# Two more units ahead of the first level of the linear attention

## What is computed

```python
def step(s, inp):
    qc, kc, vc, gc = inp
    b = jnp.cumsum(gc, axis=2)
    rel = jnp.where(lower, b[:, :, :, None, :] - b[:, :, None, :, :], -jnp.inf)
    a = jnp.einsum('bhid,bhjd,bhijd->bhij', qc, kc, jnp.exp(rel))
    o = jnp.einsum('bhid,bhde->bhie', qc * jnp.exp(b), s) + jnp.einsum('bhij,bhje->bhie', a, vc)

def _merge(o_att, o_gla, r, glu, gates, p):
    o_gla = _rmsnorm(o_gla, p['gla_norm']).transpose(0, 2, 1, 3).reshape(B, L, GLA_V)
    y_gla = (o_gla * jax.nn.silu(r)) @ p['w_gla_o']
    g_att, g_gla, g_conv = jnp.split(jax.nn.sigmoid(gates), N_BRANCH, axis=-1)
    return (g_att * y_att + g_gla * y_gla + g_conv * y_conv) @ p['w_out']
```

## Time and profile before

| | us |
|---|---|
| median of 3 runs | 3085.33 (3079.8 to 3087.47) |
| the profiled execution, its time | 3074.02 |
| its span, from first to last instruction | 3072.2 |
| TensorE busy | 2873.4 (94%) |
| VectorE busy | 2202.6 (72%) |
| ScalarE busy | 1507.7 (49%) |
| granted TensorE clock, mean | 0.953 of full speed |

### The profile page before, as it was taken

How to read it: one execution, slowest core, us unless ns; L and a number is a source line. 1 busy time by engine, 2 the same in 40 slices (tenths; PEclk the granted TensorE clock), 3 DMA queues, 4 the chain that set the end, 5 groups by cost and what they waited for, 6 DMA issues and landing times.

```text
span 3072.2 us, 54612 instructions
## 1 busy us (share of the span) xinstructions
PE 2873.4 (94%) x21460; PEld 2728.1 (89%) x21460; DVE 2202.6 (72%) x3789; ACT 1507.7 (49%) x3102; POOL 0.2 (0%) x4
## 2 busy tenths in 40 slices
PE   8999999999899999989998999998999889997998
PEld 7998889899889879989988997897998779995998
DVE  6976777678799876866657898867666655566655
ACT  3644345444555434545465653454544455555554
POOL 0000000000000000000000000000000000000000
PEclk7999989899999989989999999998999899998999
DMA  7543434388543233435533423335453326541554
GB/s 265 155 158 102 142 121 157 130 279 274 190 157 111 96 104 130 145 116 179 182 125 112 150 77 110 110 118 189 151 185 117 110 64 191 186 140 48 163 181 156
DMA packets 123191, 451.50 MB, mean 147 GB/s; under 512 B 13728, under 2 KB 15776, under 8 KB 122192
## 3 DMA queue, kind: packets, MB, share of 16 engines
q1 hardware_dynamic: 108704, 393.35, 39.5%
q10 hardware_dynamic: 14256, 54.86, 5.3%
HBM read 447.10 MB, written 1.05 MB: 146 GB/s over the span
## 4 chain that ended last, share of the span: by engine, by line
PE 64%; DVE 23%; ACT 5%; DMA 5%; issue 2%; SPq 0%; ACTq 0%; DVEq 0%
PE lin L467 14%; PE lin L468 14%; PE lin L469 14%; DVE w_lo L1588 6%; DVE arena L1759 5%; DMA w_raw<-in_stream 4%; PE lin L517 3%; PE aux L580 2%; ACT w_hi L1023 2%; PE aux L712 1%; DVE rstd L1613 1%; PE aux L571 1%; PE aux L645 1%; PE aux L624 1%; PE lin L480 1%
## 5 line engine op out<-in xcount | busy, mean ns | idle before, releaser
L1588 DVE TENSOR_TENSOR w_lo<-w_raw,w_hi 128x1024 fp32r<-128x1024 f32 x722 | 876.3, 1221 | 334.0 <-ACT w_hi L1023 330.2
L467 PE MATMUL lin<-h_hi,w_hi 128*128 128x256 f32 x3584 | 1033.3, 288 | 7.4 <-ACT arena L1280 3.7
L468 PE MATMUL lin<-h_lo,w_hi 128*128 128x256 f32 x3584 | 1022.0, 285 | 0.0
L469 PE MATMUL lin<-h_hi,w_lo 128*128 128x256 f32 x3584 | 1021.7, 285 | 0.0
L1023 ACT ACTIVATE w_hi<-w_raw 128x512 fp32r<-128x512 f32 x1446 | 828.5, 623 | 320.1 <-DMA w_raw<-in_stream 228.4
L467 PEld LDWEIGHTS lin<-h_hi,w_hi 128*128 128x128 f32 x3584 | 696.4, 194 | 13.8 <-ACT arena L1280 5.9
L468 PEld LDWEIGHTS lin<-h_lo,w_hi 128*128 128x128 f32 x3584 | 696.4, 194 | 0.4
L469 PEld LDWEIGHTS lin<-h_hi,w_lo 128*128 128x128 f32 x3584 | 695.7, 194 | 0.0
L467 PE MATMUL lin<-s_hi,w_hi 128*128 128x256 f32 x1392 | 411.9, 296 | 17.1 <-DVE s_lo L1674 13.7
L468 PE MATMUL lin<-s_lo,w_hi 128*128 128x256 f32 x1392 | 403.6, 290 | 0.0
L469 PE MATMUL lin<-s_hi,w_lo 128*128 128x256 f32 x1392 | 403.0, 290 | 0.0
(11 more groups left out here) (269 smaller groups left out, 3963.9 us busy)
## 6 DMA issues: line engine op xcount, KB each, us to landing
w_raw<-in_stream SPq DMA_DIRECT2D x723, 512.0 KB, 3.5
a_raw<-in_ada ACTq DMA_DIRECT2D x58, 512.0 KB, 3.4
arena<-in_rows ACTq DMA_DIRECT2D x38, 512.0 KB, 5.6
arena<-in_first SPq DMA_DIRECT2D x2, 2048.0 KB, 19.7
X<-in_tokens SPq DMA_DIRECT2D x2, 1024.0 KB, 14.7
s_f<-in_ada SPq DMA_DIRECT2D x4, 512.0 KB, 10.5
arena<-in_ada SPq DMA_DIRECT2D x4, 512.0 KB, 17.3
arena<-in_const ACTq DMA_DIRECT2D x1, 1856.0 KB, 9.3
```

What stands on the lines that cost most here:

```text
L467: used(pe.matmul(o, whi, hi[:, k, :], start=k == 0, stop=False), first)
L468: pe.matmul(o, whi, lo[:, k, :], start=False, stop=False)
L469: mm = pe.matmul(o, wlo, hi[:, k, :], start=False, stop=k == kcs - 1)
L1588: dve.tensor_tensor(w_lo[:, m % SLOTS, :], w_raw[:, m % RAW, :], w_hi[:, m % SLOTS, :].bitcast(F32), ALU.subtract).then_inc(sems["lo_ready ...
```

## The change

Place 0 of each of the three full passes takes the first three units of `gla_fill` (LEAD = 2 more than one), and the rest is dealt over the other sixteen places.

```diff
+LEAD = 2
+
+
 def gla_steps(l, s):
 
-    steps = spread(gla_fill(l, s), STEPS)
+    units = gla_fill(l, s)
+    rest = spread(units[LEAD + 1:], STEPS - 1)
+    steps = [units[:LEAD + 1]] + rest
     if s == CTX:
         for k, u in enumerate(STATE_UNITS):
             steps[HAT_STEP + 5 + k // 2].append(u)
```

## The result

| | before | changed |
|---|---|---|
| median of 20 runs each, us | 3079.89 (3068.32 to 3087.47) | 3090.03 (3078.66 to 3100.76) |
| ratio, with its 95% interval | | 1.0033 (1.002 to 1.0045) |
| span of the profiled execution, us | 3072.2 | 3076.8 |
| granted TensorE clock, mean | 0.953 | 0.953 |

The medians differ by 10.1 us, where the forecast was 10.6. The kernel is slower by 0.33%; the interval lies wholly above 1. The time itself was forecast at 3096 us, 6 above the 3090.0 measured: the forecast stood on a median of three runs, 3085.3, and that of twenty is 3079.9.

The account below looks back on a forecast made before the run. TensorE was taken to bound most context places and VectorE the later latent places. Context +3.2 and two latent passes +7.4 gave +10.6 us: 3084.6 on the profiled execution, 3096 us on the median, range 3085 to 3104.

Parts of the forecast that it names:

- What bounds a latent pass: Later latent places hang on VectorE, not TensorE; work moved ahead returns only as far as VectorE's own work shrinks.
- Rival 2: First wait is won for good because VectorE has slack later: -10.4 us, 3075 us; chance 0.05.
- Place 0: Latent passes: two more units bring 5.7 us forward but delay the product 3.8; gain 1.9, wait 2.0 left.
- The late load: Weight loads at place 0: costed at nothing; without the cover of earlier waiting, one would be late by under 1 us.
- Places 6 and 11: Latent places left without a unit: TensorE waits 2.2 and 3.05 us; the places save 0.7 and 1.1 us.
- The clock in a latent pass: Falls to clock 0.50 behind the three new waits: two falls at 1.5 us, +3.0, ends 0 and +4.6.
- all of the longest and half of the other two: Latent passes: counts a sure fall behind the 3.05 us wait, half each behind 2.0 and 2.2: two falls.
- VectorE busy without a gap from place 7 on: Sign expected in the latent passes of the profile after the change.
- Rival 1: Clock holds through waits of about 2 us: only +5 us, 3090 us; chance 0.22.
- The context pass: Waits grow from 3.8 to 6.1 us, +2.3; with the clock falls, +3.2 us (0.6 to 5.7).
- The half fall more: Context pass: three and a half stretches at the lower clock taken after the change, against three before.
- Rival 3: Falls feed each other, above all in context places 7 to 10: +17 to +25 us, about 3105 us; chance 0.11.

Follow-up runs that it names:

- the filled kernel: Changed kernel with throw-away matmuls filling TensorE's waits at latent places 0, 6, 11 and context places 0, 8, 10: 3085.61 us against 3078.51 for the kernel before, ratio 1.0019.
- the kernel with late subtractions: Changed kernel, but in latent passes VectorE does the two added subtractions after place 0's multiplications: 3086.47 us against 3078.74 for the kernel before, ratio 1.0029.
- The three filled kernels: Throw-away matmuls in TensorE's waits of the changed kernel, the kernel before, and one with a hand-dealt context pass: ratios to before 1.0019, 1.0006, 1.0001.

## Why the prediction was right

The forecast of +10.6 us met the difference of the medians, 10.1. The mechanism that it gave, VectorE's order in the latent passes and the clock behind new waits, is the one that the runs show. That the sum came within 0.5 us is luck in part, since two of its terms are off in opposite directions.

- **What bounds a latent pass: right.** What is put ahead of VectorE's multiplications at place 0 is late to the end, save what VectorE's own shorter places give back. Rival 2, that the first wait is won for good, fell: with the clock at 1.00 in both kernels a latent pass is still 2.19 us longer.
- **Place 0: right.** The first product was forecast 8.3 us behind the scan with a wait of 2.0; it stands at 925.76 - 917.51 = 8.25 with 1.89. The late load cost nothing, as said: ScalarE waited 0.94 us for it (925.24 above), and VectorE's next subtraction had no gap.
- **Places 6 and 11: right.** Waits forecast 2.2 and 3.05, measured 2.00 and 2.71; given back 0.7 - 0.3 = 0.4 and 1.1, measured 0.44 and 1.14. With the fall of before taken out, the forecast was +0.7; 85.82 - 85.05 = +0.77.
- **The clock in a latent pass: the mechanism right, the term too small.** Forecast +3.0, from two falls of 1.5; measured 3.87, from three, the later ones 1.4 and 1.0. The latent pass was forecast at +3.7 and cost 4.65 in the first pair of profiles. The step that failed is "all of the longest and half of the other two": in the six latent passes that have the change as it stands, 17 of 18 such waits were followed by clock 0.50. The later falls reach the path through ScalarE and VectorE: in the latent pass of layer 0 VectorE waits for ScalarE 0.85 and 0.44 us behind the second fall (to 961.34 and 967.89) and 0.77 behind the third (to 987.88), and the filled kernel has none of these waits. So the prediction's sign "VectorE busy without a gap from place 7 on" did not come. Rival 1, that the clock holds through waits of 2 us, is out for this kernel as it stands. The rule of the Trainium skill on long idle stretches (TensorE: Matmul & The Clock Gate, section "HAM oscillation — how this bites in real kernels") doesn't describe these: here waits of 1.89, 2.00 and 2.71 us were followed by clock 0.50, so the measurement decides.
- **The context pass: too large.** Forecast +3.2, measured +1.8 in the first pair of profiles. The waits were forecast at +2.3 and came to +1.4: place 0 had 1.76, which is 3.45 less the 1.7 of the chunk, where the prediction wrote 1.9; place 7 (0.4) had none, though 0.31 us in three of the six executions below; place 8 had 2.23 instead of 2.4, place 10 had 0.74 instead of 1.4, and two waits for a chunk's DMA of 0.21 and 0.26 were not thought of, which came at the chunks of places 7 and 10. The half fall more didn't come. Over six executions of the new context pass (119.03 to 122.88, mean 121.68) and three of the old (121.12, 121.14, 122.44, mean 121.57) the difference is 0.1 us, with 6.8 us at half clock on the mean against 11.4. So the new arrangement has more waiting there and fewer falls, and the forecast had both going up.
- **The sum.** Over the same executions a latent pass costs 89.49 - 85.29 = 4.2 us. 2 x 4.2 + 0.1 = 8.5 us, within the interval of the result, 6.2 to 13.9 us. Against these means the forecast was 0.5 too low in each latent pass and 3.1 too high in the context pass: the sum is closer than its parts.

Rival 3, falls that feed each other, was not seen: the context pass had at most three stretches after the change, and in the kernel before up to four.

## What to carry to other kernels

Before work is put into one engine's wait, look at what the same unit queues on the engine that is waited for: here 5.7 us of TensorE's work went into a wait of 3.9 us, but its two subtractions, and a wait for the high part that they need, went ahead of the release. 3.8 us of delay followed, of which the places left empty gave back 1.6. Each empty place also left TensorE a new wait of 2.0 or 2.7 us, and the clock fell behind 11 of 12 of these, at 1.0 to 1.4 us each. And where the clock moves by itself, compare the lengths of the stages touched and time the whole in many runs: one profile of the whole would here have shown 4.6 or 16.2 us for a loss of 10.

## What the runs showed of the hardware

- **The length of a wait alone does not decide whether the clock falls.** The wait of 2.00 us at place 6 was followed by 0.50 in six of six latent passes of the change, and the one of 2.71 in five of six; in the kernel with late subtractions, which has no wait at place 0 and one of 0.55 to 1.22 at place 1, the same two waits were followed by it in three of eight cases. The wait of 2.23 us at place 8 of the context pass had no fall right behind it in any of six executions, whereas one began within 0.8 us behind the wait at place 10, of 0.74 to 1.19 us, in four of them. And the wait of 0.26 us near the end of the context pass (at some 270 us) was followed by one within 1.5 us in three of twelve executions. What else decides is open.
- **Falls taken away in the stages are not missing from the whole span.** The three filled kernels have 7 to 10 us at half clock in their stages, where the kernels before and changed have 17 to 31. In the whole span they have 286.7, 298.2 and 300.5 us, against 290.2 and 297.1 of the kernel before, and the rest of their spans, 2789.7 to 2796.8, is longer than that of all nine others, 2774.6 to 2789.1. That filling one wait makes falls elsewhere is what these numbers suggest; with one profile each it isn't shown, and no run here tells why.
